# Depthwise convolutions of q, k and z with the running sum of their taps kept in PSUM

## The chip, the cores and the metric

The kernel runs on one core of one Trainium2 chip. The metric is the device time of the whole kernel in microseconds (us), from the runs without the profiler. One further execution was taken with the profiler, and everything that is read from a trace below comes from it.

## What is computed

The input has 512 tokens of 1024 channels. Two transformer-like blocks follow each other. The first one projects the normalised tokens and runs a short depthwise convolution along the tokens over the columns of z, its two gates, q and k. After it come a long convolution (Hyena), a bidirectional mLSTM, cross attention over 256 memory tokens and a feed-forward layer. The second block has a convolution branch, an LRU branch and a gated feed-forward layer. What matters here is the short convolution:

```python
def _short_conv_centred(u, w, b):
    L = u.shape[1]
    up = jnp.pad(u, ((0, 0), (1, 1), (0, 0)))
    return up[:, :L] * w[0] + up[:, 1:L + 1] * w[1] + up[:, 2:] * w[2] + b

# in first_block
proj = _rms_norm(h, norm_mix_g[l]) @ w_in[l]
hy = _short_conv_centred(proj[..., :HY_COLS], hy_conv_w[l], hy_conv_b[l])        # z and its gates, 1536 columns
qk = jax.nn.silu(_short_conv_centred(proj[..., HY_COLS:off], ml_conv_w[l], ml_conv_b[l]))   # q and k, 1024 columns
```

## The kernel before

All products with weights are float32 work done in three passes. A weight strip is 128 x 1024 values (`raw`, 512 KB from HBM). SyncE loads it into one of four slots (line 496), and a slot is free again when TensorE has finished the strip that lay in it (`pe_done`). ScalarE copies the strip into its high part `w_hi` (line 1155), GpSimd subtracts to get the low part `w_lo` in two instructions of 128x512 (line 515), and only then does TensorE multiply: eight blocks of three matmuls (lines 560 to 562), 24 matmuls for a strip, into one PSUM bank of 128 x 512 float32.

Each engine has one queue, and the order in it is written out by hand. Semaphores tie the queues together. `pe_done` counts finished strips; `evac` counts banks that VectorE has emptied; `conv` and `z_conv` count convolutions that are done; `m_w` counts weight tiles of the mLSTM.

**The q and k strips.** After one strip for the gates (bank 2) come eight strips, `S_QK + u`, in bank (u + 3) % 4. From u = 3 on, strip u starts only when the bank of strip u - 4 is empty (`taken=E_GATE + u - 2`). VectorE's part is `qk_convolved(u)`, lines 1856 to 1869. It scales the bank by `rstd` into the padded strip `pbuf`, and this instruction gives the bank back. It then forms the middle tap plus the bias in `s0`, adds the first tap in `s1`, and adds the third tap in `cbuf`, which ScalarE turns into q or k with a SiLU (line 1331). All of these are in SBUF. Between qk_convolved(0) and qk_convolved(1) VectorE works out the gates (lines 1898 to 1911). Between the fourth and fifth it waits for `gMH`, which ScalarE makes behind the SiLU of strip 3 (line 1348), and computes `gML` (line 1916).

**The z strips.** Twelve strips, `S_Z + m`, go to banks 3 and 2 in turn. The helper `blocks(first, end)` on TensorE runs them one block of three matmuls at a time, and before block 0 of strip m it waits for `evac` at E_Z + m - 1. For m = 1 and more that is the last user of its bank. For m = 0 it is strip 6 of q and k, though bank 3 was last used by strip 4. VectorE's part is `z_convolved(m)`, lines 1918 to 1936, with the same four steps (scratch `ctmp` and the second half of `cbuf`). The last tap is two instructions of 256 columns, the second of which writes the second half of the tokens in reverse order. TensorE then transposes `cbuf` (line 702, `z_turn(m)`), and ScalarE keeps the result.

**The order around them.** From z strip 2 on, TensorE alternates between blocks of z strips and the 32 steps of the mLSTM: a product of q and k (line 779, which waits until VectorE has weighed the step before the last), every four steps a row of exponents (line 752) and every four steps the outputs of a unit (line 768). VectorE alternates in the same way between `weigh(n)` (lines 1951 and 1956) and `z_convolved(m)`, which is placed behind the step in which TensorE finishes strip m:

```python
            for n in range(STEPS):
                weigh(n)
                if n % TT == 1 and n > TT:
                    outputs(n // TT - 1)
                ...
                for m in range(1, N_Z):
                    if m < N_Z - 1 and min(first_step((m + 1) * KT) + 1, STEPS - 1) == n:
                        z_convolved(m)
```

z_turn(0) stands behind the first blocks of strip 2, z_turn(m - 1) before the last block of strip m, and z_turn(11) behind the first products of the long convolution. The memory's keys follow it.

Of the kernel before, what the change touches and what calls it, by code (L numbers as in the profile page):

```python
# [31 lines left out]
ALU = mybir.AluOpType  # L32
# [4 lines left out]
T = 512  # L37
TT = T // P
HALF = T // 2
# [34 lines left out]
E_QK = E_GATE + N_GATE  # L74
E_Z = E_QK + N_QK
# [84 lines left out]
def build(nc, A, out):  # L160
    ctx = ExitStack()
    with ctx:
        def at(name, cols, offset, dt=F32):
            return nc.alloc_sbuf_tensor_at("m_" + name, [P, cols], dt, offset=SBUF0 + offset)

        def sem(name):
            return ctx.enter_context(nc.semaphore(name))
# [34 lines left out]
        cbuf = at("cbuf", 2 * T, 188 * KB + 128)  # L202
        ctmp = at("ctmp", T, 46 * KB)
        pbuf = at("pbuf", T + 2, 192 * KB + 5632)
# [61 lines left out]
        rstd = at("rstd", T, small + 7712)  # L266
        s0 = at("s0", T, small + 9760)
        s1 = at("s1", T, small + 11808)
# [5 lines left out]
        def col(name, k=0, rows=P):  # L274
            return const[0:rows, COL[name] + k:COL[name] + k + 1]
# [4 lines left out]
        ps = ctx.enter_context(nc.psum_tensor("ps", [P, 8, T], F32))  # L280
# [27 lines left out]
        evac = sem("evac")  # L308
# [48 lines left out]
        conv = sem("conv")  # L357
        vo_kept = sem("vo_kept")
        qk_free = sem("qk_free")
        z_conv = sem("z_conv")  # L360
# [1319 lines left out]
        def _(dve):  # L1680
            ch = Chain(dve, dchain)
# [139 lines left out]
            m = [misc[:, 8 * i:8 * i + 8] for i in range(8)]  # L1821
# [34 lines left out]
            def qk_convolved(u):  # L1856

                dve.wait_ge(pe_done, S_QK + u + 1)
                if u:
                    dve.wait_ge(conv, u)  # L1860
                dve.tensor_tensor(pbuf[:, 1:T + 1], ps[:, (u + 3) % 4, :], rstd[:], ALU.mult).then_inc(evac, 1)
                dve.wait_ge(evac, E_QK + u + 1)
                ch.add(dve.tensor_scalar(s0[:], pbuf[:, 1:T + 1], col("qc1", u), col("qcb", u), ALU.mult, ALU.add))
                ch.sync()
                ch.add(dve.scalar_tensor_tensor(s1[:], pbuf[:, 0:T], col("qc0", u), s0[:], ALU.mult, ALU.add))
                ch.sync()
                dve.wait_ge(qk_free, u + 1)
                dve.scalar_tensor_tensor(cbuf[:, (u % 2) * T:(u % 2 + 1) * T], pbuf[:, 2:T + 2], col("qc2", u), s1[:],
                                         ALU.mult, ALU.add).then_inc(conv, 1)

            def rows(buf, d):

                r = buf[g, d * T:(d + 1) * T]
                return r[:, ::-1] if d else r
# [19 lines left out]

            dve.scalar_tensor_tensor(gX[g, :], gF[g, :], -1.0, gF[g, :], ALU.mult, ALU.max).then_inc(g_abs, 1)
            qk_convolved(0)
            dve.wait_ge(g_ln, 1)
            ch.add(dve.scalar_tensor_tensor(gY[g, :], gF[g, :], 0.0, gX[g, :], ALU.min, ALU.subtract))
# [13 lines left out]
            for u in range(1, N_QK):  # L1912
                qk_convolved(u)
                if u == 4:
                    dve.wait_ge(g_high, 1)
                    dve.tensor_tensor(gML[g, :], gM[g, :], f(gMH[g, :]), ALU.subtract).then_inc(g_low, 1)

            def z_convolved(m):

                dve.wait_ge(pe_done, S_Z + m + 1)  # L1920
                if m:
                    dve.wait_ge(z_conv, m)
                dve.tensor_tensor(pbuf[:, 1:T + 1], ps[:, 3 - m % 2, :], rstd[:], ALU.mult).then_inc(evac, 1)
                dve.wait_ge(evac, E_Z + m + 1)
                ch.add(dve.tensor_scalar(ctmp[:], pbuf[:, 1:T + 1], col("tc1", m), col("tcb", m), ALU.mult, ALU.add))
                ch.sync()
                ch.add(dve.scalar_tensor_tensor(cbuf[:, T:2 * T], pbuf[:, 0:T], col("tc0", m), ctmp[:],
                                                ALU.mult, ALU.add))
                ch.sync()
                if m:  # L1930
                    dve.wait_ge(z_turned, m)

                ch.add(dve.scalar_tensor_tensor(cbuf[:, 0:HALF], pbuf[:, 2:HALF + 2], col("tc2", m),
                                                cbuf[:, T:T + HALF], ALU.mult, ALU.add))
                dve.scalar_tensor_tensor(cbuf[:, HALF:T], pbuf[:, T + 1:HALF + 1:-1], col("tc2", m),
                                         cbuf[:, 2 * T - 1:T + HALF - 1:-1], ALU.mult, ALU.add).then_inc(z_conv, 1)

            dve.wait_ge(conv, N_QK)
            dve.wait_ge(qk_free, N_QK + 2)
# [1 line left out]
            dve.tensor_copy(misc[:, 0:64], ps[:, 7, 0:64]).then_inc(g_colsv, 1)  # L1941
            dve.wait_ge(g_colsv, 1)
            z_convolved(0)

            def weigh(n):
# [69 lines left out]
# [4 lines that stand above are left out]
                if n in (18, 19):  # L2019
                    two_sum(0, n - 18, z_two, 4)  # L2020
                elif n in (20, 22):
                    two_difference(0, (n - 20) // 2, z_two)
                elif n == STEPS - 4:
                    z_lows_of(0, 2)
                elif n == STEPS - 2:
                    z_lows_of(2, 1)
                    two_sum(4, 0, gates_two, 8)
# [3 lines that stand above are left out]
# [7 lines left out]

            z_lows_of(3, 1)
            z_convolved(N_Z - 1)  # L2040
            outputs(7)
            def mlstm_sums():
# [574 lines left out]
```

## Time and profile before

| what | value |
|---|---|
| median of 3 runs | 1742.68 us |
| lowest and highest | 1742.45 and 1743.74 us |
| the profiled execution, its time | 1744.64 us |
| the profiled execution, its span from first to last instruction | 1742.8 us |
| TensorE busy, share of the span | 97% |
| VectorE busy | 51% |
| ScalarE busy | 37% |
| GpSimd busy | 48% |
| mean granted TensorE clock | 0.994 |

The profiled execution's time is 1.84 us above its span, and 1.96 us above the median of the runs. Busy time is time in which an engine worked on an instruction. A high share on TensorE says that most of the span is matmuls. It doesn't say which engine is late in a given stretch. That is read from the idle times and what ended them.

### The profile page before, as it was taken

How to read it: one execution, taken by the hardware profiler on the slowest of the kernel's cores; microseconds unless marked ns; L12 is line 12 of the kernel's file. 1: busy time of each engine (PE TensorE's matmuls, PEld its weight loads, DVE VectorE, ACT ScalarE, POOL GpSimd, SP SyncE). 2: the span in 40 equal slices, each digit the busy share in tenths (PEclk: the TensorE clock that was granted, in tenths of full speed). 3: DMA queues.
4: the chain of work that ended last, by engine and by line, in shares of the span. 5: the costliest groups of instructions: out<-in, count | busy, mean ns of one | idle time of the engine just before them, and what ended most of it. 6: DMA issues, size and time to landing. Idle time of an engine off the chain costs nothing.

```text
span 1742.8 us, 21399 instructions
## 1 busy us (share of the span) xinstructions
PE 1697.4 (97%) x7524; PEld 1372.3 (79%) x7524; DVE 890.2 (51%) x1168; ACT 653.5 (37%) x841; POOL 834.0 (48%) x610
## 2 busy tenths in 40 slices
PE   8999998889999999999999999999999999999997
PEld 5677777767877888888887888888888888888886
DVE  6869678864345715151546767663333532232234
ACT  5553333444224211111145575763333432222222
POOL 3327225775324544444445566664444444444443
PEclk9999999999999999999999999999999999999998
DMA  5122112342212222222223333332222223222222
GB/s 219 49 73 96 50 49 74 120 149 93 85 37 97 97 96 88 96 94 96 96 96 97 109 111 106 115 102 96 96 96 97 97 97 97 96 96 97 97 96 97
DMA packets 48496, 167.57 MB, mean 96 GB/s; under 512 B 5237, under 2 KB 7413, under 8 KB 48186
## 3 DMA queue, kind: packets, MB, share of 16 engines
q1 hardware_dynamic: 45728, 161.66, 27.9%
q10 hardware_dynamic: 2714, 5.17, 0.8%
q8 instruction: 36, 0.59, 0.1%
q14 instruction: 18, 0.15, 0.0%
HBM read 164.71 MB, written 2.10 MB: 96 GB/s over the span
## 4 chain that ended last, share of the span: by engine, by line
PE 45%; issue 20%; POOL 14%; DVE 1%; POOLq 0%; ACT 0%; DVEq 0%
PE ps L560 15%; PE ps L562 15%; PE ps L561 15%; POOL m_w_lo L515 14%; DVE m_h L2448 0%; POOL m_QL L533 0%; POOLq L523 0%; POOLq L521 0%; DVE m_qs L2081 0%; DVE m_s L2398 0%; PE ps L1125 0%; ACT m_QH L1441 0%; PE ps L1124 0%; PE ps L588 0%; DVE m_e L2437 0%
## 5 line engine op out<-in xcount | busy, mean ns | idle before, releaser
L515 POOL TENSOR_TENSOR m_w_lo<-m_raw,m_w_hi 128x512 fp32r<-128x512 f32 x598 | 816.8, 1388 | 876.9 <-ACT m_w_hi L1155 876.7
L1155 ACT ACTIVATE m_w_hi<-m_raw 128x1024 fp32r<-128x1024 f32 x299 | 315.5, 1057 | 608.2 <-DMA m_raw<-in_strips 608.1
L560 PE MATMUL ps<-m_XH,m_w_hi 128*128 128x512 f32 x1096 | 436.6, 398 | 1.9 <-DVE m_XL L2055 0.9
L562 PE MATMUL ps<-m_XH,m_w_lo 128*128 128x512 f32 x1096 | 427.0, 390 | 0.0
L561 PE MATMUL ps<-m_XL,m_w_hi 128*128 128x512 f32 x1000 | 389.4, 389 | 0.0
L560 PEld LDWEIGHTS ps<-m_XH,m_w_hi 128*128 128x128 f32 x1096 | 205.7, 188 | 51.8 <-issue 6.3
L562 PEld LDWEIGHTS ps<-m_XH,m_w_lo 128*128 128x128 f32 x1096 | 205.7, 188 | 43.3
L561 PEld LDWEIGHTS ps<-m_XL,m_w_hi 128*128 128x128 f32 x1000 | 187.8, 188 | 40.2 <-issue 1.7
L560 PE MATMUL ps<-m_FH,m_w_hi 128*128 128x512 f32 (+1 forms) x438 | 169.3, 387 | 0.4 <-DVE m_FL L1687 0.4
L561 PE MATMUL ps<-m_FL,m_w_hi 128*128 128x512 f32 (+1 forms) x438 | 169.1, 386 | 0.0
L562 PE MATMUL ps<-m_FH,m_w_lo 128*128 128x512 f32 (+1 forms) x438 | 169.1, 386 | 0.0
L560 PE MATMUL ps<-m_YH,m_w_hi 128*128 128x512 f32 x384 | 153.2, 399 | 0.0
L562 PE MATMUL ps<-m_YH,m_w_lo 128*128 128x512 f32 x384 | 151.6, 395 | 0.0
L561 PE MATMUL ps<-m_YL,m_w_hi 128*128 128x512 f32 x384 | 151.6, 395 | 0.0
L560 PEld LDWEIGHTS ps<-m_FH,m_w_hi 128*128 128x128 f32 x438 | 82.2, 188 | 17.5 <-DVE m_FL L1687 0.9
L561 PEld LDWEIGHTS ps<-m_FL,m_w_hi 128*128 128x128 f32 x438 | 82.3, 188 | 16.8
L562 PEld LDWEIGHTS ps<-m_FH,m_w_lo 128*128 128x128 f32 x438 | 82.3, 188 | 16.6
L561 PEld LDWEIGHTS ps<-m_YL,m_w_hi 128*128 128x128 f32 x384 | 72.2, 188 | 17.8 <-issue 0.7
L560 PEld LDWEIGHTS ps<-m_YH,m_w_hi 128*128 128x128 f32 x384 | 72.2, 188 | 17.7 <-issue 0.7
L562 PEld LDWEIGHTS ps<-m_YH,m_w_lo 128*128 128x128 f32 x384 | 72.1, 188 | 17.3
L2263 DVE TENSOR_TENSOR m_h<-m_h,ps 128x512 f32 x24 | 16.5, 688 | 106.1 <-PE ps L562 106.1
L2395 DVE TENSOR_TENSOR m_s<-ps,m_rstd 128x512 f32<-128x512 f32 x22 | 15.2, 691 | 97.1 <-PE ps L562 97.1
(376 smaller groups left out, 2231.1 us busy)
## 6 DMA issues: line engine op xcount, KB each, us to landing
m_raw<-in_strips SPq DMA_DIRECT2D x300, 512.0 KB, 3.2
m_x_in<-in_x SPq DMA_DIRECT2D x4, 512.0 KB, 8.1
m_x_res<-in_x ACTq DMA_DIRECT2D x1, 2048.0 KB, 10.7
m_memf<-in_mem SPq DMA_DIRECT2D x1, 1024.0 KB, 15.8
m_decay<-in_decay ACTq DMA_DIRECT2D x1, 1024.0 KB, 10.5
out<-m_h SPq DMA_DIRECT2D x8, 128.0 KB, 2.0
out<-m_h ACTq DMA_DIRECT2D x8, 128.0 KB, 2.4
m_w<-in_w ACTq DMA_DIRECT2D x1, 512.0 KB, 7.4
```

The source lines that it names most:

```text
L515: nc.gpsimd.tensor_tensor(w_lo[:, c], raw[:, c], f(w_hi[:, c]), ALU.subtract).then_inc(lo_ready, 1)
L560: pe.matmul(dst, w_hi[:, c], xh, start=first, stop=False)
L561: pe.matmul(dst, w_hi[:, c], xl, start=False, stop=False)
L562: return pe.matmul(dst, w_lo[:, c], xh, start=False, stop=last)
L1155: act.activation(w_hi[:, c], raw[:, c], ACT.Copy).then_inc(hi_ready, 1)
L2263: dve.tensor_tensor(hm, hm, ps[:, u, :], ALU.add).then_inc(evac, 1)
L2395: dve.tensor_tensor(s0[:], ps[:, u, :], rstd[:], ALU.mult).then_inc(evac, 1)
```

## The change

The three sums of taps of each convolution no longer go through SBUF scratch (`s0` and `s1`, or `ctmp` and the second half of `cbuf`). They stay in the strip's own PSUM bank, which has been read into `pbuf` by then. The bank is given back (`evac`) only when the last tap has been read from it: VectorE waits for its own last instruction and raises `evac` by an instruction of its own. The number of arithmetic instructions is the same, four for a strip of q and k and five for one of z.

```diff
@@ qk_convolved(u)
-                dve.tensor_tensor(pbuf[:, 1:T + 1], ps[:, (u + 3) % 4, :], rstd[:], ALU.mult).then_inc(evac, 1)
-                dve.wait_ge(evac, E_QK + u + 1)
-                ch.add(dve.tensor_scalar(s0[:], pbuf[:, 1:T + 1], col("qc1", u), col("qcb", u), ALU.mult, ALU.add))
-                ch.sync()
-                ch.add(dve.scalar_tensor_tensor(s1[:], pbuf[:, 0:T], col("qc0", u), s0[:], ALU.mult, ALU.add))
+                bank = ps[:, (u + 3) % 4, :]
+                ch.add(dve.tensor_tensor(pbuf[:, 1:T + 1], bank, rstd[:], ALU.mult))
+                ch.sync()
+                ch.add(dve.tensor_scalar(bank, pbuf[:, 1:T + 1], col("qc1", u), col("qcb", u), ALU.mult, ALU.add))
+                ch.sync()
+                ch.add(dve.scalar_tensor_tensor(bank, pbuf[:, 0:T], col("qc0", u), bank, ALU.mult, ALU.add))
                 ch.sync()
                 dve.wait_ge(qk_free, u + 1)
-                dve.scalar_tensor_tensor(cbuf[:, (u % 2) * T:(u % 2 + 1) * T], pbuf[:, 2:T + 2], col("qc2", u), s1[:],
+                dve.scalar_tensor_tensor(cbuf[:, (u % 2) * T:(u % 2 + 1) * T], pbuf[:, 2:T + 2], col("qc2", u), bank,
                                          ALU.mult, ALU.add).then_inc(conv, 1)
+                dve.wait_ge(conv, u + 1)
+                dve.sem_inc(evac, 1)
@@ z_convolved(m)
-                dve.tensor_tensor(pbuf[:, 1:T + 1], ps[:, 3 - m % 2, :], rstd[:], ALU.mult).then_inc(evac, 1)
-                dve.wait_ge(evac, E_Z + m + 1)
-                ch.add(dve.tensor_scalar(ctmp[:], pbuf[:, 1:T + 1], col("tc1", m), col("tcb", m), ALU.mult, ALU.add))
-                ch.sync()
-                ch.add(dve.scalar_tensor_tensor(cbuf[:, T:2 * T], pbuf[:, 0:T], col("tc0", m), ctmp[:],
-                                                ALU.mult, ALU.add))
+                bank = ps[:, 3 - m % 2, :]
+                ch.add(dve.tensor_tensor(pbuf[:, 1:T + 1], bank, rstd[:], ALU.mult))
+                ch.sync()
+                ch.add(dve.tensor_scalar(bank, pbuf[:, 1:T + 1], col("tc1", m), col("tcb", m), ALU.mult, ALU.add))
+                ch.sync()
+                ch.add(dve.scalar_tensor_tensor(bank, pbuf[:, 0:T], col("tc0", m), bank, ALU.mult, ALU.add))
...
                 ch.add(dve.scalar_tensor_tensor(cbuf[:, 0:HALF], pbuf[:, 2:HALF + 2], col("tc2", m),
-                                                cbuf[:, T:T + HALF], ALU.mult, ALU.add))
+                                                bank[:, 0:HALF], ALU.mult, ALU.add))
                 dve.scalar_tensor_tensor(cbuf[:, HALF:T], pbuf[:, T + 1:HALF + 1:-1], col("tc2", m),
-                                         cbuf[:, 2 * T - 1:T + HALF - 1:-1], ALU.mult, ALU.add).then_inc(z_conv, 1)
+                                         bank[:, T - 1:HALF - 1:-1], ALU.mult, ALU.add).then_inc(z_conv, 1)
+                dve.wait_ge(z_conv, m + 1)
+                dve.sem_inc(evac, 1)
```

## Rows read from the trace of the kernel before

**Rows 1.** The page's first part: busy time of each engine, share of the span, instructions.
```profile
PE 1697.4 (97%) x7524; PEld 1372.3 (79%) x7524; DVE 890.2 (51%) x1168; ACT 653.5 (37%) x841; POOL 834.0 (48%) x610
```

**Rows 2.** Busy time by stretch: length, then PE, PEld, DVE, ACT, POOL, PEclk, DMA, GB/s.
```profile
184.00:274.00 90.00, 90.00 (x463) 71.08 (x461) 69.59 (x148) 29.29 (x63) 24.29 (x18) 1.00 0.16 53
```

**Rows 3.** Timeline of TensorE: start, duration, instruction, [idle before it <- what ended it].
```profile
142.52 0.39 PE L560 MATMUL ps<-m_XH,m_w_hi 128*128 128x512 f32 x1
...
159.24 0.47 PE L560 MATMUL ps<-m_XH,m_w_hi 128*128 128x512 f32 x1 [0.24 <-DVE m_pbuf L1861]
...
179.60 0.70 PE L779 MATMUL ps<-m_QK 128*128 128x256 f32 x2 [1.68 <-DVE m_W L1956]
...
183.28 0.66 PE L702 MATMUL ps<-m_const,m_cbuf 128*128 128x128 f32 x4 [0.72 <-DVE m_cbuf L1935]
...
275.93 2.50 PE L768 MATMUL ps<-m_VX,m_W 128*128 128x129 f32 x20 [1.56 <-DVE m_W L1956]
...
282.13 0.66 PE L702 MATMUL ps<-m_const,m_cbuf 128*128 128x128 f32 x4 [0.91 <-DVE m_cbuf L1935]
```

**Rows 4.** VectorE's groups by line and shape: count | busy us, mean ns | idle before.
```profile
L1927 DVE SCALAR_TENSOR_TENSOR m_cbuf<-m_pbuf,m_const,m_ctmp 128x512 f32<-128x512 f32 x12 | 10.8, 902 | 0.4
L1868 DVE SCALAR_TENSOR_TENSOR m_cbuf<-m_pbuf,m_const,m_s 128x512 f32<-128x512 f32 x8 | 9.7, 1209 | 0.3
L1935 DVE SCALAR_TENSOR_TENSOR m_cbuf<-m_pbuf,m_const,m_cbuf 128x256 f32<-128x256 f32 x12 | 8.8, 734 | 0.0
```

**Rows 5.** The same view, three groups that read PSUM elsewhere in the kernel.
```profile
L1718 DVE TENSOR_SCALAR m_s<-ps,m_const 128x512 f32<-128x512 f32 x1 | 0.8, 797 | 0.0
...
L2055 DVE SCALAR_TENSOR_TENSOR m_XL<-ps,m_const,m_XH 128x512 fp32r<-128x512 f32 x4 | 2.8, 742 | 1.0 <-ACT m_XH L1521 1.0
...
L1750 DVE TENSOR_TENSOR m_sd_a<-ps,m_decay 128x1024 f32<-128x1024 f32 x4 | 4.9, 1220 | 0.4 <-PE ps L607 0.2
```

**Rows 6.** Timeline of VectorE and ScalarE in the stage of q and k.
```profile
138.46 0.67 DVE L1861 TENSOR_TENSOR m_pbuf<-ps,m_rstd 128x512 f32<-128x512 f32 x1
...
147.69 1.67 DVE L1868 SCALAR_TENSOR_TENSOR m_cbuf<-m_pbuf,m_const,m_s 128x512 f32<-128x512 f32 x1
...
153.26 1.04 ACT L1348 ACTIVATE m_gMH<-m_gM 4x1024 fp32r<-4x1024 f32 x1
...
155.47 0.67 DVE L1861 TENSOR_TENSOR m_pbuf<-ps,m_rstd 128x512 f32<-128x512 f32 x1
156.18 0.55 DVE L1863 TENSOR_SCALAR m_s<-m_pbuf,m_const 128x512 f32<-128x512 f32 x1
...
157.55 0.75 DVE L1868 SCALAR_TENSOR_TENSOR m_cbuf<-m_pbuf,m_const,m_s 128x512 f32<-128x512 f32 x1
...
158.40 0.69 DVE L1861 TENSOR_TENSOR m_pbuf<-ps,m_rstd 128x512 f32<-128x512 f32 x1
```

**Rows 7.** Timeline of VectorE at z_convolved(1), (10) and (11).
```profile
180.25 0.68 DVE L1923 TENSOR_TENSOR m_pbuf<-ps,m_rstd 128x512 f32<-128x512 f32 x1
...
183.14 0.28 DVE L1951 TENSOR_TENSOR m_ex<-m_ex,m_const 128x128 f32<-128x128 f32 x1
...
268.68 0.69 DVE L1923 TENSOR_TENSOR m_pbuf<-ps,m_rstd 128x512 f32<-128x512 f32 x1
...
272.87 0.28 DVE L1951 TENSOR_TENSOR m_ex<-m_ex,m_const 128x128 f32<-128x128 f32 x1
...
277.18 0.69 DVE L1923 TENSOR_TENSOR m_pbuf<-ps,m_rstd 128x512 f32<-128x512 f32 x1
```

**Rows 8.** TensorE's timeline at two later waits.
```profile
293.39 0.50 PE L560 MATMUL ps<-m_ZH,m_w_hi 128*128 128x512 f32 x1 [2.07 <-POOL m_w_lo L515]
...
350.18 0.50 PE L560 MATMUL ps<-m_ZH,m_w_hi 128*128 128x512 f32 x1 [2.70 <-POOL m_w_lo L515]
```

**Rows 9.** Busy time by stretch behind the first of these waits, columns as above.
```profile
294.00:296.00 2.00, 2.00 (x6) 1.56 (x5) 0.07 (x1) 2.00 (x3) 2.00 (x1) 0.50 0.10 41
296.00:298.00 2.00, 2.00 (x8) 1.58 (x7) 1.22 (x2) 1.09 (x8) 2.00 (x3) 0.65 0.00 0
```

## Prediction

> **What bounds the kernel now.** I read the page's shares first: TensorE is busy 97% of the span and VectorE 51% [rows 1]. VectorE's time therefore counts only where TensorE waits for it. Next come the stretches. From 184 to 274 us, where z_convolved(2) to z_convolved(10) lie, TensorE is busy 90.00 of 90.00 us [rows 2]. Nothing that VectorE saves there moves the end. Then the timeline of TensorE, for the waits that VectorE ends around the twenty convolutions. There are five [rows 3], each the idle time before the row named. At 159.24 z strip 0 waited 0.24 us for the bank of q/k strip 6. At 179.60 a product waited 1.68 us for weigh(0), at 183.28 z_turn(1) waited 0.72 us for z_convolved(1), at 275.93 the last outputs waited 1.56 us for weigh(31), and at 282.13 z_turn(11) waited 0.91 us for z_convolved(11). Last come VectorE's groups: the sum on line 1868 has a mean of 1209 ns and that on line 1927 of 902 ns [rows 4]. Single rows show that these means mix two durations: line 1868 takes 0.75 us at 157.55 and 1.67 us at 147.69 [rows 6].
>
> **What the change does to one convolution.** It takes no instruction away. It changes the memory of three operands and moves one signal.
>
> Price of the tensor_scalar: it runs in 0.55 us from SBUF to SBUF [rows 6]. With PSUM as its source and two column operands it takes 0.80 us [rows 5]. I take 0.80 for PSUM as its destination, since the nearest row has the same operands and differs only in the direction. Lower end: 0.55, no change. That is +0.25 us per convolution.
>
> Price of the sums: a scalar_tensor_tensor with one PSUM input, a column operand and 512 columns takes 0.74 us [rows 5], and 0.75 is what I take for both. No row shows an instruction that reads and writes one bank. The upper bound is a second stream of 512 columns for it: 1024 columns from PSUM take 1.22 us [rows 5] against 0.69 for 512 [rows 6], so +0.53 us for the one in-place sum.
>
> The slow versions go. Lines 1868, 1927 and 1935 read two SBUF tensors, and their means [rows 4] hold instances of over twice the short time [rows 6]. The scaling from PSUM and `rstd`, with one SBUF input, takes 0.67 and 0.69 us [rows 6]. With a bank as the other input all sums have that form, so I take the undisturbed durations everywhere. The Trainium skill (SBUF — State Buffer, "Who interferes with whom") gives the reason: only a VectorE instruction with two SBUF inputs or in a two-port mode locks out GpSimd or is locked out.
>
> Against the change speaks the Trainium skill's cycle table (VectorE: DVE Perf Modes, on the trn2 errata), which starts a PSUM source at 120 cycles and an SBUF source at 58. By it each of the two sums would cost an estimated 0.065 us more, 0.13 per convolution, and the sum of the steps below about 0.9 us higher. The rows show no such step: the same form takes 0.74 us with a PSUM source [rows 5] and 0.75 us with SBUF alone [rows 6].
>
> Pace of a q/k convolution: from 155.47 to 158.40 is 2.93 us undisturbed [rows 6]. After the change 2.93 + 0.25 + 0.05 for the added signal instruction = 3.23. The 0.05 is an estimate from the ends and starts around it (0.05 to 0.15 us). Of a z convolution: from 180.25 to 183.14 is 2.89 us [rows 7]. There the next instruction, line 1951, started before the last tap had ended. The new wait forbids that, and I take 0.20 for it and the signal: 2.89 + 0.25 + 0.20 = 3.34. Queued behind this wait are weigh(n) and the units' outputs, and TensorE waits for those. Between 184 and 274 us it found them ready [rows 2].
>
> **Where it reaches the path.** Times are of the profiled execution.
>
> 1. z strip 0. It waits for `evac` of q/k strip 6, which was raised by the first instruction (158.40 + 0.69 = 159.09, TensorE started at 159.24) and will be raised behind the last. VectorE's q/k run starts at 138.46 [rows 6], ended by gate work that stays. With a pace of 3.23, strip 3's convolution (the third from there) ends at 138.46 + 3 x 3.23 - 0.15 = 148.0, where it was 147.69 + 1.67 = 149.36 [rows 6]. ScalarE's `gMH` follows that SiLU at a fixed distance and ends at 154.30 - 1.36 = 152.94. Strip 4's convolution ends at 151.2, before it. `gML` puts strip 5 at 155.47 - 1.36 = 154.11, strip 6 at 157.34, and its last tap ends 3.11 us later at 160.45. With 0.05 for the signal and 0.15 to TensorE, z strip 0 starts at 160.65: +1.4 us. Strips 5 to 7 still start later than their banks come free. The nearest is strip 5, whose bank comes free at 138.46 + 3.23 = 141.7, when strip 1 is done. TensorE started strip 5 at 142.52 [rows 3], so this wait has 0.8 us of cover.
> 2. z_turn(1). TensorE already waits there for z_convolved(1), undisturbed before. The dearer tensor_scalar adds 0.25: +0.25. The wait at 179.60 hangs on strip z 1 by its load, ScalarE's copy and the exponent, so it moves along and stays as long.
> 3. The last outputs. VectorE is the late one from weigh(28) on, and z_convolved(10) lies between. It took 272.87 - 268.68 = 4.19 us [rows 7] and will take 3.34: -0.85 of the 1.56 us idle.
> 4. z_turn(11). z_convolved(11) ran from 277.18 [rows 7] to 282.08. Its successor takes 3.3 us. The products before z_turn(11) end with TensorE idle 0.91 us, all of which goes, since VectorE would now be done 0.7 us before TensorE: -0.9.
>
> Sum: 1.4 + 0.25 - 0.85 - 0.9 = -0.1 us. Behind it TensorE starts the memory's keys 0.1 us earlier. The waits for `w_lo` (2.07 and 2.70 us idle [rows 8]) come from a slot that TensorE frees there, so they keep their length. VectorE is up to 0.65 us ahead, which I count at nothing: it meets the same slots. If GpSimd's order shifts there, it is worth up to 0.5 us either way.
>
> For the profiled execution that is 1744.64 - 0.1, span 1742.7. Against the median of the runs, 1742.68, it makes 1742.6.
>
> **Rivals.**
>
> *In-place sums stream twice.* Each convolution costs 0.53 us more. z strip 0 has five convolutions in its chain (three before `gMH`, two behind): 1.4 + 5 x 0.53 = 4.05. z_turn(1): 0.25 + 0.53 = 0.78. The last outputs: -0.85 + 0.53 = -0.32. z_turn(11): it ends 0.53 + 0.53 later against a cover of 0.7, so -0.5. Sum +4.0, 1746.7 us, slower by 0.23%. It decides from about 0.5 us per convolution upwards. For it: no row shows the form. Against it: reading PSUM costs nothing extra in any row.
>
> *The new wait costs clock.* Behind the 2.07 us without work before 293.39 the granted clock was 0.50 in one stretch of 2 us and 0.65 in the next [rows 8, 9]: 1.2 in place of 2.4 GHz for about 3.4 us. The new idle at z strip 0 is 0.24 + 1.4 = 1.65 us, near the 1.56 and 1.68 us of rows 3, behind which TensorE lost none, while 2.70 us idle at 350.18 [rows 8] lost none either. So it depends on more than the length of the gap. A dip of 3.4 us at half speed costs 1.7: sum +1.6, 1744.3 us.
>
> *VectorE's time counts in full.* The sums lose their slow instances: 9.7 - 8 x 0.75 = 3.7 us on line 1868, 10.8 - 12 x 0.75 = 1.8 on line 1927 and, with 0.75 - 0.53/2 = 0.48 for half the columns, 8.8 - 12 x 0.48 = 3.0 on line 1935 [rows 4], 8.5 us in all. The 20 dearer tensor_scalars take back 5. If the late signal cost nothing and TensorE were given the rest, it would be -3.5 us, 1739.2, and all 8.5 would be 1734.2. Against it stand the 90.00 us without a gap [rows 2].
>
> *The change doesn't do what it says*: the sums are as slow beside GpSimd as before, or the tensor_scalar stays at 0.55. The second gives 0.15 + 0 - 1.1 - 0.9 = -1.85 us, 1740.8. The first keeps the idle at 275.93 and 282.13 and delays z strip 0 by some 3.5 us more: about +6 us, 1748.7.
>
> **How the numbers follow.** A measurement of this kernel can tell about 0.2%, 3.5 us, from no change. Forecast (1741.6 to 1743.6): 0.60. Clock dip at the new wait or elsewhere: 0.17, same. Cheap tensor_scalar: 0.10, same. In-place sums twice as long: 0.05, slower. Sums still disturbed: 0.03, slower. VectorE counts in full, or a dip of the clock behind 293 us goes as well: 0.05, faster or same by half each. The predicted time is the forecast's, 1742.6. The range is 1740.0 to 1746.0, from the cheap tensor_scalar less some clock to a dip and part of the in-place cost. Faster 0.03, within 0.2% 0.89, slower 0.08.
>
> **What would show it.** The tensor_scalar at 0.80 us and the sums at 0.75 us with no instance above 1 us; TensorE's idle before z strip 0 at 1.65 us instead of 0.24, ended by the last tap on line 1868 or its successor; at z_turn(1) 0.25 us more idle; before the last outputs 0.7 us instead of 1.56; none before z_turn(11). I would be wrong if the in-place sum took over 1.2 us, if a q/k strip (5 first) waited for its bank, or if the gain at 276 and 282 us were lost again in the long convolution, whose waits for `w_lo` I have taken as fixed.

## The result and the profile after

| what | before | after |
|---|---|---|
| median | 1742.87 us (20 runs) | 1745.56 us (20 runs) |
| lowest and highest | 1740.75 and 1744.49 us | 1741.40 and 1747.18 us |
| profiled execution, time and span | 1744.64 and 1742.8 us | 1745.57 and 1743.8 us |
| mean granted TensorE clock | 0.994 | 0.993 |

The ratio of the runs is 1.0015, with a 95% interval from 1.0009 to 1.0021. The changed kernel is 2.7 us slower. That is inside the 0.2% that I called no change and inside my range, yet the interval doesn't hold 1, and my sum of -0.1 us is wrong.

The page's first part shows the gain where I looked for it. VectorE is busy 7.6 us less than in [rows 1] and GpSimd 7.1 us less. The kernel as a whole didn't get faster by it.

```profile
PE 1699.8 (97%) x7524; PEld 1374.6 (79%) x7524; DVE 882.6 (51%) x1168; ACT 653.2 (37%) x841; POOL 826.9 (47%) x610
```

VectorE's groups by line and shape (count | busy us, mean ns | idle before) stand against [rows 4]. The tensor_scalar into PSUM takes 814 ns and the in-place sum 756 ns. The last taps take 748 ns, or 481 and 475 ns for half the columns. The mean on line 1869 was 1209 ns, and now no instance is slow.

```profile
L1929 DVE TENSOR_SCALAR ps<-m_pbuf,m_const 128x512 f32<-128x512 f32 x12 | 9.8, 814 | 0.4
L1931 DVE SCALAR_TENSOR_TENSOR ps<-m_pbuf,m_const,ps 128x512 f32<-128x512 f32 x12 | 9.1, 756 | 0.4
...
L1869 DVE SCALAR_TENSOR_TENSOR m_cbuf<-m_pbuf,m_const,ps 128x512 f32<-128x512 f32 x8 | 6.0, 748 | 0.3
...
L1936 DVE SCALAR_TENSOR_TENSOR m_cbuf<-m_pbuf,m_const,ps 128x256 f32<-128x256 f32 x12 | 5.8, 481 | 0.4
L1938 DVE SCALAR_TENSOR_TENSOR m_cbuf<-m_pbuf,m_const,ps 128x256 f32<-128x256 f32 x12 | 5.7, 475 | 0.0
L1862 DVE TENSOR_TENSOR m_pbuf<-ps,m_rstd 128x512 f32<-128x512 f32 x8 | 5.5, 689 | 1.1 <-DVE m_cbuf L1869 1.1
```

The last line holds what I had priced too low. VectorE sat idle 1.1 us in all before the next scaling, and its own last tap ended that idle. VectorE's timeline (start, duration, instruction, [idle before it <- what ended it]) shows each instance, here the convolutions of strips 5 to 7:

```profile
154.50 0.67 DVE L1862 TENSOR_TENSOR m_pbuf<-ps,m_rstd 128x512 f32<-128x512 f32 x1
...
157.81 0.69 DVE L1862 TENSOR_TENSOR m_pbuf<-ps,m_rstd 128x512 f32<-128x512 f32 x1 [0.21 <-DVE m_cbuf L1869]
...
160.18 0.75 DVE L1869 SCALAR_TENSOR_TENSOR m_cbuf<-m_pbuf,m_const,ps 128x512 f32<-128x512 f32 x1
161.14 0.69 DVE L1862 TENSOR_TENSOR m_pbuf<-ps,m_rstd 128x512 f32<-128x512 f32 x1 [0.21 <-DVE m_cbuf L1869]
```

The pace from strip 6 to 7 is 161.14 - 157.81 = 3.33 us (3.31 to 3.34 between the other strips), where I had 3.23.

TensorE's timeline at the waits of [rows 3] and [rows 8]:

```profile
161.13 0.47 PE L560 MATMUL ps<-m_XH,m_w_hi 128*128 128x512 f32 x1 [1.98 <-DVEq L1872]
...
162.16 0.63 PE L560 MATMUL ps<-m_XH,m_w_hi 128*128 128x512 f32 x1
...
183.12 0.70 PE L779 MATMUL ps<-m_QK 128*128 128x256 f32 x2 [1.69 <-DVE m_W L1961]
...
187.06 0.66 PE L702 MATMUL ps<-m_const,m_cbuf 128*128 128x128 f32 x4 [0.97 <-DVE m_cbuf L1938]
...
278.92 2.50 PE L768 MATMUL ps<-m_VX,m_W 128*128 128x129 f32 x20 [0.77 <-DVE m_W L1961]
284.06 0.60 PE L702 MATMUL ps<-m_const,m_cbuf 128*128 128x128 f32 x4
...
295.13 0.50 PE L560 MATMUL ps<-m_ZH,m_w_hi 128*128 128x512 f32 x1 [1.95 <-POOL m_w_lo L515]
...
311.95 0.80 PE L560 MATMUL ps<-m_QH,m_w_hi 128*128 128x512 f32 x1 [2.63 <-POOL m_w_lo L515]
```

z strip 0 waited 1.98 us for the new signal (line 1872) in place of 0.24. Right behind that its matmuls take 0.63 us in place of 0.39. Busy time by stretch (length, then PE, PEld, DVE, ACT, POOL, PEclk, DMA, GB/s) names the cause: a granted clock of 0.52 and 0.62, that is 1.2 GHz in place of 2.4 for 3.4 us.

```profile
161.50:163.50 2.00, 2.00 (x7) 1.53 (x6) 1.91 (x3) 0.10 (x1) 0.32 (x1) 0.52 0.18 59
163.50:165.50 2.00, 2.00 (x7) 1.64 (x6) 0.75 (x1) 1.20 (x2) 0.00 (x0) 0.62 0.00 0
165.50:167.50 2.00, 2.00 (x10) 1.64 (x10) 0.00 (x0) 0.38 (x1) 1.55 (x2) 1.00 0.00 0
```

I worked out the account from the starts of the same matmuls in both timelines. Each column of the table is the time from the start of one to the start of the next, in us, and a kernel's row is one execution. The first row of before is the execution whose rows stand ahead of the prediction. The marks are q/k strip 2 (125.76 us before), z strip 0 (159.24), the first matmul behind its 24 (164.86), the last outputs (275.93), the memory's keys (282.55), the first matmul behind the wait of 1.17 us at 310.26, and a later strip of the long convolution's stage (393.72).

| kernel | q/k 2 to z 0 | z 0 | to outputs | to keys | sum to keys | to 310 | to 394 | falls of the clock from 284 to 394 us |
|---|---|---|---|---|---|---|---|---|
| before | 33.48 | 5.62 | 111.07 | 6.62 | 156.79 | 27.72 | 83.46 | 294, 335, 379 |
| before, again | 33.46 | 5.65 | 111.36 | 6.62 | 157.09 | 27.61 | 82.40 | 297, 338 |
| after | 35.23 | 7.24 | 110.55 | 5.50 | 158.52 | 27.53 | 85.18 | 312, 339, 353, 390 |
| after, again | 35.21 | 7.24 | 110.57 | 5.48 | 158.50 | 27.77 | 84.61 | 313, 340, 354, 384 |

From q/k strip 2 to the keys the change costs 158.52 - 156.79 = 1.7 us. That is 1.75 at the wait, 1.62 by the clock in strip 0, -0.52 up to the last outputs and -1.12 up to the keys. Another 85.18 - 83.46 = 1.7 us appear between 310 and 394 us, in a stretch that holds no changed instruction. The two spans differ by only 1.0 us, since the profiled execution of before had a longer end: 1742.8 - 1731.09 = 11.7 us behind the start of its seventh last matmul, against 1743.8 - 1734.23 = 9.6 after (9.5 in before's second trace). The extra time lies in the output's transfers and the last instructions, which the change doesn't touch. Between the matmul at 394 us and that seventh last matmul the four traces take 1337.0 to 1337.4 us, so nothing else differs there. The medians, 2.7 us apart, are the better measure.

### The profile page after: what moved, and what is told of

Its sections match the earlier page's. It is cut to its first block, busy times and chain, and to the rows that moved or that the text cites. A ratio compares the mean times of both kernels' runs of the same rounds, so it can differ in the third digit from the quotient of the medians.

```text
span 1743.8 us, 21419 instructions
## 1 busy us (share of the span) xinstructions
PE 1699.8 (97%) x7524; PEld 1374.6 (79%) x7524; DVE 882.6 (51%) x1168; ACT 653.2 (37%) x841; POOL 826.9 (47%) x610
## 4 chain that ended last, share of the span: by engine, by line
PE 46%; issue 32%; POOL 20%; DVE 1%; DMA 0%; POOLq 0%; ACT 0%; DVEq 0%; SPq 0%
POOL m_w_lo L515 19%; PE ps L560 15%; PE ps L562 15%; PE ps L561 15%; POOL m_QL L533 1%; DMA m_raw<-in_strips 0%; DVE m_h L2453 0%; DVE m_ZL L2042 0%; DVE m_qs L2114 0%; POOLq L523 0%; POOLq L521 0%; POOL m_w_lo L539 0%; DVE m_s L2403 0%; DVE m_s L2107 0%; DVE m_qs L2113 0%
## 6 DMA issues: line engine op xcount, KB each, us to landing
m_decay<-in_decay ACTq DMA_DIRECT2D x1, 1024.0 KB, 10.2
```

## The experiments

My theory after reading the result, called A in the quoted texts: the late signal makes z strip 0 wait 2 us, and the clock falls right behind that wait and makes it 1.6 us dearer. The rivals put the loss elsewhere: in the z convolutions and their in-place sums, in the wait alone so that the clock plays no part, or in falls of the clock that come by chance. Each quoted text says in its own words what it tests. The 95% interval behind each ratio reaches some 1.6 us either way (2.3 us for the late wait with its 5 runs), so that no single median can carry a difference below that. The stretches read from the traces repeat better.

**Wait for the bank that is needed.** z strip 0 takes bank 3, last used by q/k strip 4, but waits for strip 6.

```diff
-                        pe.wait_ge(evac, E_Z + m - 1)
+                        pe.wait_ge(evac, E_Z + m - 1 if m else E_Z - 3)
```

> The changed kernel, but z strip 0 waits only for the bank that it takes (bank 3, last used by q/k strip 4) and no longer for q/k strip 6. Theory A (the loss is the wait at z strip 0, made longer by the drop of TensorE's clock right behind it): z strip 0 follows q/k strip 7 without idle time, no drop of the clock there; TensorE is 1.9 us ahead of the kernel before at the memory's keys, so about 1741.0 us, ratio 0.999. Theory B (the sums in PSUM and the added signal cost time all over the stage, the wait at z strip 0 is a small part): at least 1744 us, ratio 1.0006 or more.

Measured: 1741.55 us (12 runs), ratio to the kernel before 0.9990 [0.9982, 0.9999]. In the trace strip 0 starts without idle time, the strip takes 5.53 us and the clock doesn't fall.

```profile
160.69 0.39 PE L560 MATMUL ps<-m_XH,m_w_hi 128*128 128x512 f32 x1
```

The stretch up to the keys takes 154.68 us, 3.8 less than in the changed kernel (158.52) and 2.3 less than before (156.94, the mean of its two traces, against which the stretches below are held too). All in-place sums and all signals behind the convolutions are still in. So neither the sums nor the z convolutions make the loss.

**Keep TensorE at work during the wait.** Ahead of strip 0's wait stand seven more matmuls of 512 columns into a bank that nobody uses there. They don't shorten the wait.

```diff
+                        if m == 0:
+                            for _ in range(7):
+                                pe.matmul(ps[:, 5, :], w_hi[:, n % RING * STRIP:n % RING * STRIP + P], tile(XH, 0),
+                                          start=True, stop=True)
                         pe.wait_ge(evac, E_Z + m - 1)
```

> The changed kernel with seven additional matmuls of 512 columns into the unused bank 5, put before the wait of z strip 0: they take about 1.6 us of the 2.0 us in which TensorE would stand idle, and their result is used nowhere. Theory A: z strip 0 starts when it did (161.1 us), the granted clock stays at full speed behind it, its 24 matmuls take 5.3 us instead of 6.9; 1.6 us are won, about 1744.0 us, ratio 1.0006. Theory C (the drop of the clock comes anyway, or its cost is made up for later): ratio unchanged at 1.0015, 1745.6 us.

Measured: 1743.44 us (11 runs), 1.0000 [0.9991, 1.0009]. TensorE's timeline has the filling (1.75 us) and the strip behind it:

```profile
161.01 1.75 PE L724 MATMUL ps<-m_XH,m_w_hi 128*128 128x512 f32 x7
163.04 0.50 PE L560 MATMUL ps<-m_XH,m_w_hi 128*128 128x512 f32 x1 [0.28 <-DVEq L1876]
...
163.61 0.40 PE L562 MATMUL ps<-m_XH,m_w_lo 128*128 128x512 f32 x1
```

Strip 0 starts as late as after the change, 35.13 us behind q/k strip 2 against 35.23. Only the idle time is gone, up to the 0.28 us that are left. The strip then takes 5.67 us instead of 7.24, and the granted clock stays at 1.00:

```profile
163.00:165.00 2.00, 1.96 (x9) 1.62 (x10) 1.79 (x3) 0.59 (x1) 0.85 (x1) 1.00 0.47 178
165.00:167.00 2.00, 2.00 (x10) 1.68 (x9) 1.22 (x2) 0.71 (x2) 0.00 (x0) 1.00 0.00 0
```

This separates the two halves of theory A. The wait costs 1.75 us, and the clock costs 1.6 more because TensorE has nothing to do in it.

**Take the signal off VectorE.** TensorE waits on the convolutions' own counts (`conv`, `z_conv`), and VectorE neither waits for itself nor signals behind a convolution. The old counter is caught up once at the end of each part.

```diff
-                dve.wait_ge(conv, u + 1)
-                dve.sem_inc(evac, 1)
...
-                        pe.wait_ge(evac, E_Z + m - 1)
+                        pe.wait_ge(*((z_conv, m - 1) if m > 1 else (conv, N_QK - 1 + m)))
```

> The changed kernel with TensorE waiting on the counts of finished convolutions (conv, z_conv) instead of evac; the wait and the signal instruction behind each convolution are gone, evac is raised once for all eight and once for all twelve. Operands as in the changed kernel. Theory A: each q/k convolution is 0.11 us shorter, z strip 0 waits 1.3 to 1.5 us instead of 2.0 us; 0.6 us won with a drop of the clock there (1744.9 us), about 2.3 us without it (1743.3 us). Theory B: more than 2 us won even where the drop stays.

Measured: 1741.74 us (11 runs), 0.9990 [0.9981, 0.9999]. The idle time is 1.58 us instead of 1.98, and the clock doesn't fall behind it:

```profile
161.35 0.47 PE L560 MATMUL ps<-m_XH,m_w_hi 128*128 128x512 f32 x1 [1.58 <-DVE m_cbuf L1869]
```

The stretch up to the keys takes 156.21 us, 2.3 less than after the change. VectorE's pace is 3.22 us without them:

```profile
158.09 0.69 DVE L1862 TENSOR_TENSOR m_pbuf<-ps,m_rstd 128x512 f32<-128x512 f32 x1
...
161.31 0.69 DVE L1862 TENSOR_TENSOR m_pbuf<-ps,m_rstd 128x512 f32<-128x512 f32 x1
```

Strip 0 starts 34.83 us behind q/k strip 2 in place of 35.23. Signal and wait thus add about 0.4 us at z strip 0: 0.11 us in each of three steps of VectorE's chain, and the rest at the hand-over to TensorE. In this one trace the 1.6 us of clock stayed away together with that 0.4 us. The time came out 1.6 us below the 1743.3 us that A had for this case.

**Each half alone.** In the first of the two only z's convolutions are changed, in the second only those of q and k.

> Only the z convolutions are changed; those of q and k are as before. Theory A: the wait at z strip 0 is 0.24 us as before, no drop of the clock there; z_turn(1) waits 0.3 us more, the last outputs 0.8 us and z_turn(11) 0.9 us less: 1.4 us faster than before, about 1741.5 us, ratio 0.9992. Theory B: slower than before by 0.5 us or more, since twelve of the twenty convolutions are changed.

Measured: 1742.59 us (11 runs), 0.9995 [0.9986, 1.0004]. The interval holds A's 0.9992, but also no change and B's 0.5 us.

> Only the convolutions of q and k are changed; those of z are as before. Theory A: the wait of 2.0 us and the drop of the clock stay, the gain of 1.8 us in the z stage goes: about 4.4 us slower than before, 1747.3 us, ratio 1.0025. Theory B: slower by less than the whole change, under 1.0015.

Measured: 1745.90 us (11 runs), 1.0012 [1.0003, 1.0021]. By the time alone this ratio speaks for B, which had under 1.0015, and not for A's 1.0025. The traces decide between them. Up to the keys z alone takes 155.18 us, a gain of 1.8, and q and k alone take 160.16, a loss of 3.2. In the second the gain of the z stage is gone (111.07 us to the last outputs and 6.63 to the keys, as before the change), strip 0 waits 1.98 us, and the clock falls again, all as A says:

```profile
161.00:163.00 2.00, 2.00 (x5) 1.61 (x6) 1.93 (x3) 0.43 (x1) 0.65 (x1) 0.51 0.43 162
163.00:165.00 2.00, 2.00 (x7) 1.53 (x7) 1.06 (x2) 0.87 (x2) 0.00 (x0) 0.64 0.00 0
```

The whole loss up to the keys lies in q and k. A's 1747.3 us was too high because it took the changed kernel's whole 2.7 us as its base, with the part behind the keys, and this kernel's stretch from 310 to 394 us is a short one (82.08 us).

**The late wait without the PSUM sums.** The kernel before, with z strip 0 held until the last tap of q/k strip 6:

```diff
+                        if m == 0:
+                            pe.wait_ge(conv, N_QK - 1)
```

> The kernel before with one added wait: z strip 0 waits until the whole convolution of q/k strip 6 is done. The sums stay in SBUF. Theory A: the last tap of strip 6 ends at 163.1 us beside GpSimd, so TensorE idles 4.3 us and not 2.0; with a drop of the clock behind it 4.1 + 1.6 = 5.7 us in this stage, nothing given back at 276 and 282 us: 1748.6 us, ratio 1.003. It would show that the signal's place alone costs the time and that the undisturbed sums halve the wait. Theory B: less than 2 us, since the PSUM operands cost the rest.

Measured: 1749.42 us (5 runs), 1.0034 [1.0021, 1.0048]. The idle time is 4.17 us and the strip at half clock takes 8.11 us.

```profile
163.92 0.76 PE L560 MATMUL ps<-m_XH,m_w_hi 128*128 128x512 f32 x1 [4.17 <-DVE m_cbuf L1870]
```

With the sums in SBUF strip 0 starts 37.40 us behind q/k strip 2. With the sums in PSUM it was 35.23 in the changed kernel, and 34.83 with the signal by conv, which waits on the same counter as this one. So the sums in SBUF make this wait 2.2 to 2.6 us longer. The change of memory is a gain in this chain, and the place of the signal is the loss.

**Both traces again**, to see which parts are the kernel's and which the execution's.

> The changed kernel once more, for a second trace. Theory A: TensorE again idles 2.0 us before z strip 0 with a drop of the clock behind it; from q/k strip 2 to the memory's keys 158.5 us as before. Theory D (the drops of the clock fall by the phase of each execution, not by the kernel): the drop behind z strip 0 is absent this time, the stage takes 156.9 us, and the number and places of the drops between 284 and 394 us differ from the first trace.

> The kernel before once more, for a second trace. Its stage from q/k strip 2 to the memory's keys takes 156.8 us again. Theory A has the stretch from the keys to the first stretch without waits (1668th matmul) at 111.2 us again; theory D has other drops of the clock there, and 1 to 3 us more or less.

Measured: 1746.23 and 1743.11 us, one execution each; their rows stand in the table above. After the change the idle time ahead of strip 0 is 1.98 us again and the clock falls right behind it again:

```profile
162.50:164.50 2.00, 2.00 (x7) 1.54 (x6) 1.89 (x4) 0.06 (x1) 0.28 (x1) 0.52 0.18 61
164.50:166.50 2.00, 2.00 (x7) 1.57 (x6) 0.73 (x1) 1.24 (x2) 0.00 (x0) 0.62 0.00 0
```

The stages up to the keys repeat within 0.1 us after and within 0.3 us before. In the four traces with 1.98 us or more idle at this place (both of the changed kernel, q/k alone, the late wait) the clock fell four times. The other half of A's expectation failed: in before's second trace the stretch from the keys to the matmul at 394 us takes 110.0 us and not 111.2 again, and it has one fall of the clock fewer between 310 and 394 us, as the rival D has it for this stretch.

**Signal and bank together.** The third experiment, and strip 0 waits for the convolution of the strip whose bank it takes.

```diff
-                        pe.wait_ge(*((z_conv, m - 1) if m > 1 else (conv, N_QK - 1 + m)))
+                        pe.wait_ge(*((z_conv, m - 1) if m > 1 else (conv, (N_QK - 3, N_QK)[m])))
```

> As e3_signal_by_conv (TensorE waits on the convolutions' own count, VectorE neither waits nor signals behind each), and besides strip 0 of z waits for the convolution of q/k block N_QK-4, whose bank it takes, no longer for the last but one. Theory A (the signal and the early wait for a bank that isn't needed make the loss): both savings are there at once. The idle ahead of strip 0 of z goes from 1.58 us in e3 to under 0.3 us, as in e1 (0.28 or less), no halving of the granted clock near 161 us, and the stretch from the start of q/k block 2 to the start of the keys takes 156.2 - 1.5 = 154.7 us or a little less, against 158.5 in the changed kernel and 154.68 in e1. Time 1741.0, ratio to the kernel before 0.9988. Rival (the banks that come free set the pace anyway, so that an earlier start of strip 0 only moves the wait to strip 1 of z): the idle shows ahead of strip 1 and the stretch stays at 156.2 us, time 1741.7.

Measured: 1740.71 us (11 runs), 0.9988 [0.9979, 0.9997], and 154.45 us up to the keys, with no idle time ahead of strip 0. What A expected of the trace held; the wait did not move to strip 1.

**Turn strip 1 of z a strip later.** As before this one, and `z_turn(1)` stands behind strip 2's last block.

```diff
-                    if k == KT - 1 and m > 1:
+                    if k == KT - 1 and m > 2:
                         z_turn(m - 1)
...
+                        if m == 2:
+                            z_turn(1)
```

> e7_signal_and_bank with the transposition of z's strip 1 put behind the last block of strip 2, so that TensorE doesn't wait 0.97 us for VectorE's convolution there. If TensorE's path sets the end of this stretch: the 0.97 us at 187 us go and the stretch from q/k block 2 to the keys takes 0.7 to 0.9 us less than in e7, 153.9 us; time 1740.4. Rival (a wait elsewhere takes it up, at the outputs' projection, where TensorE waits for the same convolutions, or at the next strip's bank): the stretch stays within 0.2 us of e7's and the time within 0.3 us of it.

Measured: 1739.50 us (11 runs), 0.9980 [0.9971, 0.9989]. The row with `[0.97 ...]` at z_turn(1) is there in the kernel before this one (first row below) and has lost its wait here (second):

```profile
182.66 0.66 PE L703 MATMUL ps<-m_const,m_cbuf 128*128 128x128 f32 x4 [0.97 <-DVE m_cbuf L1936]
```

```profile
183.65 0.66 PE L703 MATMUL ps<-m_const,m_cbuf 128*128 128x128 f32 x4
```

The stretch up to the keys takes 153.74 us, 0.7 less. The median fell by 1.2 us, which the noise of two medians doesn't tell from 0.7. By the medians this version is 3.4 us faster than the kernel before and some 6 us faster than the changed one.

**The stretch from 310 to 394 us.** All traces have the same work there, yet it lasts between 81.9 and 85.4 us.

| kernel | sum to keys | to 310 | to 394 | falls of the clock from 284 to 394 us | median less that of before |
|---|---|---|---|---|---|
| true bank | 154.68 | 27.58 | 83.41 | 293, 331, 348, 378 | -1.5 |
| filled wait | 156.80 | 27.50 | 81.90 | 331, 352, 379 | +0.4 |
| filled wait, again | 157.51 | 27.56 | 83.51 | 297, 338, 382 | |
| signal by conv | 156.21 | 27.70 | 83.75 | 350, 384 | -1.3 |
| z only | 155.18 | 27.59 | 85.39 | 310, 337, 350, 381 | -0.4 |
| z only, again | 155.21 | 27.62 | 84.80 | 309, 336, 350, 380 | |
| q/k only | 160.16 | 27.62 | 82.08 | 298, 339 | +2.8 |
| late wait | 163.53 | 27.66 | 83.81 | 302, 343, 357, 388 | +6.4 |
| signal and bank | 154.45 | 27.70 | 85.09 | 307, 335, 348, 386 | -2.2 |
| turn later | 153.74 | 27.69 | 83.23 | 292, 333, 377 | -3.4 |

The falls at 348 (true bank), 384 (signal by conv), 381 (z only) and 388 us (late wait) last 6.8 us, the others 3.4.

> e4_z_only once more, for one question: whether the stretch of long convolutions from about 310 to 394 us, which took 85.4 us in e4's trace and 85.2 and 84.6 in the changed kernel's two traces, against 83.5 and 82.4 in the two of the kernel before, is longer because z's change is in. If it is: over 84.5 us again. If the falls of the granted clock in it come as they please: between 82 and 85.5 us, and no sign of the change in it. The stretch up to the keys 155.2 us as before (within 0.2). Time 1742.6.

> e2_filled_wait once more, for the same question from the other side: its z part is the changed kernel's, yet its stretch from 310 to 394 us took 81.9 us. If z's change lengthens that stretch, 81.9 was a stray and this trace shows over 84 us; if the falls of the clock come as they please, anything from 82 to 85.5 us. The idle ahead of strip 0 of z under 0.4 us, no halving of the clock between 155 and 175 us, and 156.8 us up to the keys (within 0.2) again. Time 1743.4.

Measured: 1742.43 and 1745.77 us, one execution each. The stretch took 84.80 us in the one and 83.51 in the other, so neither half of the expectation holds as a rule for all: z alone has a long stretch twice, and the filled wait gave 81.9 and then 83.5. The second also had a fall at 184.1 us, behind an idle time of 1.84 us, which made its stages up to the keys 0.7 us longer.

What goes with the long stretch can be seen in the table. In the five traces of 84.6 us and more (both of the changed kernel, both of z alone, signal and bank) the clock did not fall behind the wait near 294 us but at the next one, at 307 to 313 us, and then twice more close together (the latter also with the true bank and with the late wait, whose stretches took 83.4 and 83.8 us). The first trace of the filled wait and that of signal by conv had a fall at neither of the two waits. Where it fell near 294 us (at 302 in the late wait, whose stages lie later), the time up to 310 is the same: TensorE works at half clock and then waits less for GpSimd, 1.17 us in before against 2.63 in after. That fall is free. At the next wait there is no such cover. From the matmul behind it to the one behind the wait that follows, near 330 us, the five traces with a fall there take 20.6 to 20.8 us and the nine others 19.2 to 19.4, so this fall costs 1.2 to 1.6 us. Before the change the end of this stretch is the first row, after it the second, at 329.61 - 310.26 = 19.35 and 332.74 - 311.95 = 20.79 us:

```profile
329.61 0.39 PE L560 MATMUL ps<-m_NH,m_w_hi 128*128 128x256 f32 x1 [2.08 <-POOL m_w_lo L515]
```

```profile
332.74 0.38 PE L560 MATMUL ps<-m_NH,m_w_hi 128*128 128x256 f32 x1 [2.03 <-POOL m_w_lo L515]
```

The changed kernel's clock at the start of it:

```profile
312.00:314.00 2.00, 2.00 (x5) 1.62 (x6) 2.00 (x2) 1.06 (x1) 2.00 (x2) 0.50 0.09 27
314.00:316.00 2.00, 2.00 (x8) 1.59 (x7) 1.97 (x3) 0.00 (x0) 2.00 (x2) 0.70 0.00 0
```

and the kernel before:

```profile
310.00:312.00 2.00, 1.74 (x8) 1.44 (x9) 1.97 (x3) 0.17 (x1) 2.00 (x3) 1.00 0.79 262
312.00:314.00 2.00, 2.00 (x14) 1.80 (x13) 1.97 (x2) 1.06 (x1) 2.00 (x2) 1.00 0.03 8
```

Which of the two waits the fall takes is not settled. The wait near 294 us is as long where it fell (2.07 us before, 1.98 in its second trace) as where it didn't (1.95 after, 2.19 in its second trace). That this accounts for the changed kernel's remaining 1 us (2.7 us by the medians, 1.6 by the stages up to the keys) and for z alone (-0.4 against -1.8) fits, but it rests on one or two traces each and no experiment forced it. Both differences are also within the noise of the medians: the changed kernel's interval goes from 1.6 to 3.7 us. Signal and bank has a long stretch too, and its median (-2.2) is within 0.3 us of its stages (-2.5); with 1.6 us either way it can't decide.

The granted clock of all runs gives one more sign. Its mean is 0.9942 over 70 runs of the kernel before, 0.9927 over 20 of the changed kernel and 0.9933 over 11 of z alone. (1 - clock) times the span, on the mean, is 10.2, 12.7 and 11.7 us. One fall of 3.4 us at half clock makes 1.7 of it. Of the changed kernel's additional 2.6 us the fall behind z strip 0 explains 1.7, and about 0.9 (standard error 0.5) is left. z alone has 1.5 us more (standard error 0.7) with no fall at strip 0 in its two traces. So runs with z's change had somewhat more of the low clock elsewhere. These runs don't show where, nor what each fall cost.

## Why the prediction was wrong, step by step

*Prices of the instructions.* Right. The tensor_scalar takes 0.814 us against 0.80 and the sums 0.748 and 0.756 against 0.75. The rival of a second stream for the in-place sum is out (756 ns, not 1.28 us), and so is the cheap tensor_scalar. My argument against the second stream, that reading PSUM costs nothing extra in any row, was true of the sums alone: the tensor_scalar takes 0.797 us from PSUM [rows 5] and 0.55 from SBUF [rows 6]. The Trainium skill's cycle table (VectorE: DVE Perf Modes, on the trn2 errata), which starts a PSUM source dearer than an SBUF one, would make the sums an estimated 0.065 us longer; they took 748 and 756 ns against 0.75 us with SBUF alone [rows 6]. The slow instances are gone in every group.

*Pace of a q/k convolution.* The first step that failed, by its size. I took 0.05 us for "the added signal instruction". It costs 0.11: VectorE stands idle 0.21 us before the next scaling where it was 0.10 (158.40 less the end of the row at 157.55 [rows 6]). The wait for the last tap was there before too, ahead of each scaling from the second on; new are the signal and a second wait for the same count ahead of it. The instructions themselves took 0.29 us more and not 0.25, as the pace of 3.22 us without the signal shows. So the pace is 3.33, not 3.23. z strip 0's chain has three such steps from one convolution to the next (to the second and third, and from strip 5 to 6): 3 x 0.11 = 0.33 us, which is the whole of 1.98 - 1.65. The shorter sums ahead of it worked as forecast but for these steps: the gates' mask (line 1348) begins at 152.28, 1.0 us earlier than in [rows 6], where I had 1.36. Two of the steps make 0.2 of the difference, and q/k strip 2 starts 0.14 us later in this trace than in before's.

*The clock at the new wait.* The second step, and the largest. I had the mechanism and its price as a rival (3.4 us at half speed, 1.7 us; measured 1.62), and gave it 0.17. I set it aside because waits of 1.56 and 1.68 us lost no clock [rows 3]. That the forecast of 1.65 us lay at the edge of these rows should have told me that an error of 0.3 us in the wait can decide on 1.6 us. In the runs, 1.58 us at this place (signal by conv, one trace) lost no clock, 1.98 us lost it in three traces of three and 4.17 us in one of one. Where the forecast lies between a row that loses nothing and one that does [rows 8, 9], the odds can't be 0.60 to 0.17.

*z_turn(1).* Right: 0.97 us idle against 0.72 [rows 3], +0.25.

*The last outputs and z_turn(11).* Right: 0.77 us idle against 1.56, -0.8, and no idle time before z_turn(11) (row at 284.06). Up to the keys it is 0.2 us more than the 0.9 that I had.

*The long convolution.* "They keep their length" holds up to 310 us (27.5 to 27.8 us in all fourteen traces). From 310 to 394 us it doesn't: a term that I counted at nothing, with 0.5 us either way, varies by 3.5 us, and its long cases go with a fall behind the wait near 310 us.

*The sum.* Mine: 1.4 + 0.25 - 0.85 - 0.9 = -0.1. Measured up to the keys: 1.75 + 1.62 - 0.52 - 1.12 = +1.7 us, and the medians say +2.7. The cause of the 1.7 us is shown by the experiments; that of the last 1 us, which is within the interval, stays open.

## What to carry to other kernels

Before a release of a buffer is moved to the end of a chain, look who waits for it and whether it is the buffer that the waiter needs: here a wait for the last but one strip instead of the last user of the bank was free until the release moved, and then cost 3.4 us. An early wait of nearly 2 us on TensorE has to be priced with the clock behind it, and a length near the edge between rows with and without a fall belongs into the forecast with about even chances. Let the reader wait on the counter that the last instruction raises anyway, since a signal by an instruction of its own behind the wait cost the engine 0.1 us each time, and three of them in a chain, with the hand-over, cost the reader 0.4.

## What the hardware showed that I had not expected

- A VectorE instruction that waits for its predecessor's completion and then signals leaves the next one to start 0.21 us later. With the wait alone it is 0.10 us, in the kernel before and with the signal by conv. The 0.21 came 5 times in 5 in each of the changed kernel's two traces.
- VectorE's sums with one PSUM operand freed GpSimd as well. Its subtractions between 100 and 290 us, with the same work, took 1398 ns on the mean against 1535 (1475 with z alone, 1430 with q and k alone). First the row of before, then that of after:

```profile
L515 POOL TENSOR_TENSOR m_w_lo<-m_raw,m_w_hi 128x512 fp32r<-128x512 f32 x46 | 69.5, 1535 | 113.0 <-ACT m_w_hi L1155 113.0
```

```profile
L515 POOL TENSOR_TENSOR m_w_lo<-m_raw,m_w_hi 128x512 fp32r<-128x512 f32 x46 | 63.3, 1398 | 122.5 <-ACT m_w_hi L1155 122.5
```

- Filling a 2 us wait with useless matmuls kept the clock: strip 0 took 5.67 us instead of 7.24. It does not shorten the wait.
- A fall of the clock can be free. Behind the wait near 294 us it costs nothing (the stretch "to 310" takes 27.6 to 27.7 us with it and 27.5 to 27.8 without), since the next wait for GpSimd gets shorter by as much. The idle time at this wait was 1.94 to 2.07 us in the seven executions with a fall behind it and 1.91 to 2.19 us in the seven without, so the length of the gap alone doesn't decide.
